# Retention's values of all four heads projected at once with the tokens on the partitions, heads of three tiles, and moved pieces, in a two-layer decoder trunk

## The reference

```python
h = rms_norm(x, g_mix[l])
z = h @ w_in[l]
qa, ka, va, ga, ub, vb, qc, kc, vc, gates = split_cols(z)
qa = rotary(qa.reshape(B, S, RET_HEADS, RET_DK), pos)
ka = rotary(ka.reshape(B, S, RET_HEADS, RET_DK), pos)
ya = retention(qa, ka, va.reshape(B, S, RET_HEADS, RET_DV))
ya = rms_normalize(ya) * ret_norm_g[l].reshape(RET_HEADS, RET_DV)
ya = silu(ga) * ya.reshape(B, S, RET_W)
...
x = x + merged @ w_o[l]
h = rms_norm(x, g_ffn[l])
gate, up = jnp.split(h @ w_gate_up[l], 2, axis=-1)
x = x + (silu(gate) * up) @ w_down[l]
```

## Time and profile before

| | us |
|---|---|
| median of 3 runs | 1914.49 (1914.34 to 1914.69) |
| the profiled execution's own time | 1913.97 |
| its span in the trace | 1912.2 |
| TensorE busy | 1896.2 (99%) |
| VectorE busy | 1246.9 (65%) |
| ScalarE busy | 843.6 (44%) |

### The profile page before, as it was taken

How to read it: one execution, slowest core, us unless ns; L and a number is a source line. 1 busy time by engine, 2 the same in 40 slices (tenths; PEclk the granted TensorE clock), 3 DMA queues, 4 the chain that set the end, 5 groups by cost and what they waited for, 6 DMA issues and landing times. The chain is left out here.

```text
span 1912.2 us, 26594 instructions
## 1 busy us (share of the span) xinstructions
PE 1896.2 (99%) x10632; PEld 1700.4 (89%) x10632; DVE 1246.9 (65%) x1625; ACT 843.6 (44%) x1186; POOL 97.2 (5%) x148
## 2 busy tenths in 40 slices
PE   8999999999999999999999999999999999999999
PEld 7888888888888899899888888888888888998998
DVE  7767767745656786377577677676365667863775
ACT  5544444424334455155345444345243444542554
POOL 0000001111111000000000000011111110000000
PEclk9999999999999999999999999999999999999999
DMA  5322347777777355366333222577777773553663
GB/s 202 91 75 73 85 130 185 191 203 217 211 199 212 100 168 177 100 187 198 123 100 94 67 78 81 148 197 190 208 205 199 201 205 100 180 160 107 203 209 123
DMA packets 85897, 295.68 MB, mean 155 GB/s; under 512 B 20368, under 2 KB 20624, under 8 KB 84624
## 3 DMA queue, kind: packets, MB, share of 16 engines
q1 hardware_dynamic: 73104, 218.49, 36.6%
q0 software_dynamic: 12672, 75.51, 17.5%
HBM read 291.79 MB, written 77.66 MB: 193 GB/s over the span
## 5 line engine op out<-in xcount | busy, mean ns | idle before, releaser
L1056 ACT ACTIVATE w_high<-raw 128x1024 fp32r<-128x1024 f32 x396 | 418.0, 1056 | 787.6 <-PE bank L846 663.5
L1262 DVE TENSOR_TENSOR w_low<-raw,w_high 128x1024 fp32r<-128x1024 f32 x396 | 482.8, 1222 | 148.7 <-ACT w_high L1056 142.8
L846 PE MATMUL bank<-h_high,w_high 128*128 128x512 f32 x1408 | 544.0, 386 | 9.0 <-DVE h_low L1267 8.3
L846 PE MATMUL bank<-h_low,w_high 128*128 128x512 f32 x1408 | 534.9, 380 | 0.0
L846 PE MATMUL bank<-h_high,w_low 128*128 128x512 f32 x1408 | 534.7, 380 | 0.0
L846 PEld LDWEIGHTS bank<-h_high,w_high 128*128 128x128 f32 x1408 | 267.0, 190 | 47.1 <-issue 8.2
L846 PEld LDWEIGHTS bank<-h_high,w_low 128*128 128x128 f32 x1408 | 266.8, 190 | 38.1
L846 PEld LDWEIGHTS bank<-h_low,w_high 128*128 128x128 f32 x1408 | 267.1, 190 | 36.4
L846 PE MATMUL bank<-in_high,w_high 128*128 128x512 f32 x672 | 255.0, 379 | 0.0
L846 PE MATMUL bank<-in_low,w_high 128*128 128x512 f32 x672 | 254.7, 379 | 0.0
L846 PE MATMUL bank<-in_high,w_low 128*128 128x512 f32 x672 | 254.7, 379 | 0.0
(11 more groups left out here) (163 smaller groups left out, 2345.5 us busy)
## 6 DMA issues: line engine op xcount, KB each, us to landing
raw<-weights SPq DMA_DIRECT2D x325, 512.0 KB, 4.1
weight_sums<-weights POOLq DMA_DIRECT2D x108, 512.0 KB, 6.3
raw<-weight_sums SPq DMA_DIRECT2D x72, 512.0 KB, 3.5
weight_sums<-weight_sums POOLq DMA_DIRECT2D x36, 512.0 KB, 4.0
turned<-rows SPq DMA_DIRECT2D x3, 768.0 KB, 7.6
xT<-x_t SPq DMA_DIRECT2D x8, 256.0 KB, 5.0
decay_sb<-decay SPq DMA_DIRECT2D x8, 256.0 KB, 4.8
out_t<-xT SPq DMA_DIRECT2D x8, 256.0 KB, 6.2
```

The lines of the kernel that those rows point to most:

```text
L846: return pe.matmul(o, w, m, start=start, stop=stop)
L1056: act.activation(w_high[:, PART_SLOT[s], :, :], raw[:, s % RAW_SLOTS, :, :], ACT.Copy).then_inc(part_high_w.sem, 1)
L1262: dve.tensor_tensor(w_low[:, PART_SLOT[s], :, :], raw[:, s % RAW_SLOTS, :, :], w_high[:, PART_SLOT[s], :, :], ALU.subtract).then_inc(part_ ...
```

## The change

The values of all four retention heads are four tiles (rv, 0) to (rv, 3) in a row ahead of the heads, projected like sv with the tokens on the partitions, into the banks 7, 6, 2 and the one of the tile before (`token_bank`), and copied out by ScalarE with the norm's factor per token. They live in places 10 and 11 of in_high and in_low. The heads are three tiles, rq, rk, rg, and their later steps come one tile earlier than before, counted from rq. The last dilated head's weighing, transposes and products lie beside the rv tiles and take the regular places. The decay has two buffers, the second in the place of a gate, and the loads for heads 0 and 1 are early. GpSimd starts at (rq, 0). The first loads on SP change places (third slab ahead of the identity), and the split of the third slab stands among the first squares. In the feed-forward, sums, high and low pieces stand in other places.

```diff
@@ tiles_of_layer
+    t += [("rv", j) for j in range(HEADS)]
     for h in range(HEADS):
-        t += [("rq", h), ("rk", h), ("rv", h), ("rg", h)]
+        t += [("rq", h), ("rk", h), ("rg", h)]
@@ schedule, heads
-        if h < HEADS - 1:
-            pre[t + 11] += [("weigh", h)]
-        if h < HEADS - 1:
-            pre[t + 12] += [("ptrans", h, 0), ("ptrans", h, 1)]
+        pre[t + 11] += [("weigh", h)]
+        pre[t + 12] += [("ptrans", h, 0), ("ptrans", h, 1)]
...
-        pre[t + 3] += [("vtrans", "rv", h)]
...
-        pre[t + 3] += [("rscore", h, m) for m in range(2)]
...
-        pre[t + 4] += [("rscore", h, m) for m in range(2, BLK)]
-        pre[t + 6] += [("rpv", h), ("ocopy", h), ("square", "r", h), ("split_sq", "r", h)]
-        pre[t + 7] += [("rowstat", "r", h), ("rowstd", "r", h)]
-        post[t + 7] += [("rowinv", "r", h)]
-        post[t + 8] += [("rowscale", "r", h), ("high", "yr", h), ("low", "yr", h)]
+        pre[t + 2] += [("rscore", h, m) for m in range(2)]
+        pre[t + 3] += [("rscore", h, m) for m in range(2, BLK)]
+        pre[t + 5] += [("rpv", h), ("ocopy", h), ("square", "r", h), ("split_sq", "r", h)]
+        pre[t + 6] += [("rowstat", "r", h), ("rowstd", "r", h)]
+        post[t + 6] += [("rowinv", "r", h)]
+        post[t + 7] += [("rowscale", "r", h), ("high", "yr", h), ("low", "yr", h)]
@@ schedule, feed-forward
-    post[AT["fgate", 0, 2]] += [("input_sum", "s1"), ("input_sum", "s2"), ("part_high", "s2")]
-    post[AT["fup", 0, 2]] += [("part_low", "s2"), ("part_high", "s1")]
-    post[AT["fgate", 0, 3]] += [("part_low", "s1"), ("input_sum", "s3"), ("part_high", "s3")]
+    post[AT["fgate", 0, 2]] += [("input_sum", "s1"), ("input_sum", "s2"), ("part_high", "s2"), ("part_high", "s1")]
+    post[AT["fup", 0, 2]] += [("part_low", "s2"), ("part_low", "s1"), ("input_sum", "s3")]
+    post[AT["fgate", 0, 3]] += [("part_high", "s3"), ("input_sum", "s4"), ("part_high", "s4"), ("part_low", "s3")]
...
-    post[AT["quick", PLAIN_PAIRS, A11B11]] += [("part_low", "s3"), ("input_sum", "s4"), ("part_high", "s4")]
-    post[AT["quick", PLAIN_PAIRS, S2T2]] += [("part_low", "s4"), ("part_high", "a22"), ("part_low", "a22")]
+    post[AT["quick", PLAIN_PAIRS, A11B11]] += [("part_high", "a22")]
+    post[AT["quick", PLAIN_PAIRS, S2T2]] += [("part_low", "s4")]
+    post[AT["quick", PLAIN_PAIRS, A12B21]] += [("part_low", "a22")]
@@ build
+        decays = [decay_sb[:, :], work[:, 18, :]]
...
+            return [stat_bank, out_bank, score_bank[0], bank_of(base, AT["rv", 0] - 1)]
@@ load_decay
-                if h > 0:
-
-                    sp.wait_ge(score_taken.sem, score_taken.at(base, "rscore", h - 1, BLK - 1))
-                sp.dma_start(decay_sb[:, :], decay[h]).then_inc(decay_loaded, 16)
+                if h > 1:
+                    sp.wait_ge(score_taken.sem, score_taken.at(base, "rscore", h - 2, BLK - 1))
+                sp.dma_start(decays[h % 2], decay[h]).then_inc(decay_loaded, 16)
@@ by_token
+                if role == "rv" and j == 0:
+                    pe.wait_ge(low_ready.sem, low_ready.at(base, "yc", HEADS - 2))
+                    pe.wait_ge(std_ready.sem, std_ready.at(base, "cq", HEADS - 1))
+                    pe.wait_ge(score_taken.sem, score_taken.at(base, "scores", HEADS - 1, 2))
...
+                        if role == "rv" and k == 0 and b == BLK - 1:
+                            wait_evacuated(pe, base, i - 1)
@@ rpv
-                        pe.wait_ge(v_stored.sem, v_stored.at(base, "rv", h))
+                        if h == 0:
+                            pe.wait_ge(values_ready.sem, values_ready.at(base, "rv", BLK - 1))
...
-                            last = matmul(out_bank[:, m * P:SEQ], ret_v[:, m, :], ret_s[:, RS_OFF[m]:RS_OFF[m] + SEQ - m * P],
+                            last = matmul(out_bank[:, m * P:SEQ], ret_v[m][:, h * P:(h + 1) * P], ret_s[:, RS_OFF[m]:RS_OFF[m] + SEQ - m * P],
@@ scalar, first squares (vector alike)
+                if n == 2:
+                    split(0, SPLIT_AHEAD)
```

More of the change, by code:

```diff
@@ L306, in schedule @@
             steps.append(("main", i, 0, len(BLOCKS[i])))
-        steps += splits + pre[i] + ([("evac", i)] if TILES[i][0] != "sv" else [("token_evac",)] if i == AT["sv", HEADS - 1] else [])
+        steps += splits + pre[i] + ([("evac", i)] if TILES[i][0] not in TOKEN_ROLES else
+                                [("token_evac", TILES[i][0])] if TILES[i][1] == HEADS - 1 else [])
         steps += later + post[i]
@@ L392, in build @@
         input_sum = over("input_sum", in_low_at + 4 * row_bytes, [P, 2, 4, 2 * P], F32)
+        ret_v_rows = [over("values_high", in_high_at + 10 * row_bytes, [P, 2, SEQ], F32),
+                      over("values_low", in_low_at + 10 * row_bytes, [P, 2, SEQ], F32)]
+        ret_v = [ret_v_rows[m // 2][:, m % 2, :] for m in range(BLK)]
         work_at = nc.sbuf_base
@@ L523, in build @@
         ret_copied = signal("ret_copied", keys("ocopy"))
-        values_ready = signal("spatial_values_ready", [(b,) for b in range(BLK)])
+        values_ready = signal("values_ready", [(role, b) for role in TOKEN_ROLES for b in range(BLK)])
         ln_var = signal("ln_var_ready", [()])
@@ L668, in build, with bank_number @@
         first_gate = gates[0]
+        def bank_number(base, i):
+            return (base // STRIDE * len(TILES) + i) % 2
         def bank_of(base, i):
@@ L702, in _ @@
             for layer in range(DEPTH):
-                pool.wait_ge(tile_stored.sem, tile_stored.at(layer * STRIDE, AT["rv", 0]))
+                pool.wait_ge(tile_stored.sem, tile_stored.at(layer * STRIDE, AT["rq", 0]))
                 for n, u in enumerate(QUICK_UNITS):
@@ L785, in read_pairs @@
                     pairs_swapped, 16)
-            decay_at = {behind(("k", 1, 0)): 0} | {load_behind("rscore", h - 1, BLK - 1): h
-                                                    for h in range(1, HEADS)}
+            decay_at = {behind(("k", h + 1, 0)): h for h in range(2)}
+            decay_at |= {load_behind("rscore", h - 2, BLK - 1): h for h in range(2, HEADS)}
             sp.dma_start(first_gain[:, :], gain_first).then_inc(first_gain_loaded, 16)
@@ L888, in main @@
             def main(base, i, first, end):
-                if TILES[i][0] == "sv":
+                if TILES[i][0] in TOKEN_ROLES:
                     by_token(base, i, TILES[i][1])
                     return
-                if i >= 2 * AHEAD_OF_NORM and first == 0:
+                if i == AT["rq", 0]:
+                    wait_evacuated(pe, base, AT["rv", 0] - 2)
+                elif i == AT["rk", 0]:
+                    pe.wait_ge(values_ready.sem, values_ready.at(base, "rv", BLK - 1))
+                elif i >= 2 * AHEAD_OF_NORM and first == 0:
                     wait_evacuated(pe, base, i - (4 if i < 3 * AHEAD_OF_NORM else
@@ L1080, in _ @@
                     if kind == "split_high":
-                        split(base, *key)
+                        if base > 0 or key[-1] != SPLIT_AHEAD:
+                            split(base, *key)
                     elif kind == "fill_ahead":
@@ L1133, in _ @@
                     elif kind == "token_evac":
-                        act.wait_ge(tile_done.sem, tile_done.at(base, AT["sv", HEADS - 1]))
+                        role, = key
+                        act.wait_ge(tile_done.sem, tile_done.at(base, AT[role, HEADS - 1]))
                         act.wait_ge(rstd_ready.sem, rstd_ready.at(base, "n", 0))
                         for b in range(BLK):
-                            act.activation(sg_v[:, b, :], token_bank[b][:, :], ACT.Gelu_apprx_tanh,
-                                           scale=rs[:, b:b + 1]).then_inc(values_ready.sem, 1)
+                            dst, func = (ret_v[b], ACT.Copy) if role == "rv" else (sg_v[:, b, :], ACT.Gelu_apprx_tanh)
+                            act.activation(dst, token_bank(base, role)[b][:, :], func, scale=rs[:, b:b + 1]).then_inc(
+                                values_ready.sem, 1)
                     elif kind == "square":
@@ L1277, in _ @@
                 sum_squares(dve, 0, 0, n)
+                if n == 1:
+                    split(0, SPLIT_AHEAD)
             for base in range(0, DEPTH * STRIDE, STRIDE):
@@ L1640, in _weights @@
                 src, col, row0 = w_down[layer], t[2] * P, t[1] * FF_BLOCKS[0] * P
-            elif t[0] == "sv":
+            elif t[0] in TOKEN_ROLES:
                 for s, place, i in blocks:
                     k, at = 2 * t[1] + i // 4, i % 4 * P
-                    values = w_in[layer][k * P:(k + 1) * P, of(("sv", 0)):of(("sv", 0)) + HEADS * P]
+                    values = w_in[layer][k * P:(k + 1) * P, of((t[0], 0)):of((t[0], 0)) + HEADS * P]
                     values = values.reshape(P, 2 * P, 2).transpose(0, 2, 1).reshape(P, HEADS * P)
```

37 lines of the change are left out of this document (17 added, 20 removed).

## The result

| us | before | after |
|---|---|---|
| median of 5 runs each | 1914.49 (1913.95 to 1914.77) | 1932.06 (1928.67 to 1934.24) |
| ratio | | 1.0090, 95% interval 1.0079 to 1.0101 |
| the profiled execution, its span | 1913.97, 1912.2 | 1928.67, 1926.9 |
| mean granted clock of each run | 1.000 (the profiled one) | 0.997, 0.995, 0.996, 0.996, 0.995 |

What follows compares the result with a forecast made beforehand. TensorE, busy 1896.2 of 1912.2 us, was taken as the bound. The terms -3.5 - 0.45 - 3.2 + 3.0 + 1.7 + 14.3 = +11.9 us on 1913.97 gave 1925.8, stated as 1926.0 us, range 1920.5 to 1932.

Steps and rivals of the forecast that it cites:

- the loop: Scores of one retention head to the next: VectorE's order makes TensorE idle 3.6 us before heads 2 and 3; +14.3 us.
- the rv tile: First rv tile: TensorE waits twice, for the scores' reader and the last v tile's evacuation; +3.0 us.
- the start: Program start: third slab's split moved ahead of six squares, costed at nothing; bounds 0 to 1 us.
- the first head: Scores wait for the late rotation of rk in the first head, 0.85 us a layer; +1.7 us.
- the pieces: Reordered pieces of the feed-forward input remove TensorE waits, 1.6 us a layer; -3.2 us.
- transposes and their wait: 32 value transposes dropped, -3.5 us, and the first one's wait behind the long weighing on VectorE, -0.45 us.
- Rival (b): Between heads, VectorE keeps up and rk is rotated by the end of rg's tile; 1910 us, chance 0.05.
- (c): Loop holds in part: heads 2 and 3 wait only 1.5 to 2 us; 1919 us, chance 0.08.
- The tail that I feared at the last fup tile: Feed-forward: late evacuation of the last fup tile makes the second product wait about 0.5 us.
- rival (a): Idle times ahead of heads 2 and 3 also throttle TensorE's clock; up to 12 us more, 1938, chance 0.12.

Runs made afterwards that it cites:

- kernel 1: Changed kernel plus 14 matmuls with overwritten results, filling TensorE's idle time before the rotated k of heads 2 and 3; 1924.63 us.
- kernel 7: Against kernel 6: norm factor multiplied into the rotation tables once a layer, rotation of rq and rk reads PSUM itself; 1905.99 us.
- kernel 4: The kernel before with the moved pieces of the feed-forward alone; 1911.68 us.
- kernel 3: Changed kernel with reciprocal, scaling and split of heads 0 and 1 behind the later head's rotations, and later waits in the first rv tile; 1913.01 us.
- kernel 6: Against kernel 3: low half of the last dilated head's product moved behind the first rotation of k; 1910.85 us.
- kernel 5: Against kernel 4: third slab loaded ahead of the identity and split ahead of six squares, on VectorE ahead of the first sum; 1910.51 us.
- kernel 8: Changed kernel with the reciprocal of heads 0 and 1 computed a second time into a free place; 1947.02 us.

## Why the prediction was right, and where it fell short

The sign and the mechanism held. The number, 1926.0, is 6.1 us below the median, which lies at the very edge of the range, 0.06 us past its upper end (1932.06 against 1932.0). The sum without the clock was nearly right (kernel 1, with the clock full, 1924.6), and a term that I had put down as a rival was missing from it. That the sum came so near is in part luck: the loop, the rv tile and the start came out 2.4 to 2.8 us below the forecast, the first head and the pieces 0.8 above. Step by step, for both layers:

| term | forecast | measured | by |
|---|---|---|---|
| transposes and their wait | -3.95 | -4.0 | kernel 7, its trace |
| pieces | -3.2 | -2.9 | kernel 4 |
| first rv tile | +3.0 | +2.2 to +2.6 | kernel 3 |
| first head | +1.7 | +2.2 | kernel 6 |
| loop, heads 2 and 3 | +14.3 | +13.5 | 4 x 3.37 |
| start | 0 (0 to 1) | -1.2, likely | kernel 5, whose start differs a little |
| clock | 0 | +7.4 | kernel 1 |

The measured column makes +17.2 to +17.6; the medians differ by 17.6.

**The loop.** TensorE's part of it came out as worked out: from the first score (310.63) to the small scores on VectorE (318.38) 7.75 us. VectorE's part took 15.76 us in place of 16.07, almost all of it in the stretch from the second evacuation to the low half of yr, 4.54 (326.79 to 331.33) in place of 4.91: read from the earlier trace rows that stretch held a wait of 0.96 us for ScalarE's high half, here 0.73, and a low half of 0.83 us, here 0.69. I had taken VectorE's starts in the old order as if nothing in them were waiting; one gap travelled with them. Rival (b), that VectorE keeps up, fell with the new waits and with kernel 8, where a microsecond more on VectorE was a microsecond more of waiting; (c) fell with the four stalls of 3.37 us, where it had 1.5 to 2.

**The pieces and the rv tile.** The tail that I feared at the last fup tile is there and of the size I gave it (idle 0.52 for 0.5). The first rv tile cost less mostly because the evacuation of the v tile took 1.34 us there and not 1.52.

**The start** was the one edit costed at nothing that wasn't nothing, by what the medians of kernels 4 and 5 suggest. The profiled run of before had the third slab's low half just in time, and so its trace showed no wait; one execution does not tell whether a margin is there or luck.

**The clock** is the step that failed. As rival (a) with a chance of 0.12 the clock was treated nearly as all or nothing, and as unlikely. It was neither: kernel 1 shows 7.4 us, more than half of rival (a)'s 12. "Nothing here tried it" was an argument for not knowing, and I read it as an argument against; with idle times four times the longest seen before, even odds on rival (a)'s 12 us and a forecast near 1932 would have been the honest sum. By the Trainium skill (TensorE: Matmul & The Clock Gate, HAM oscillation) a TensorE that waits is throttled again and pays on each return. Kernel 8 agrees, 6.4 us idle and a fall at each of four; the changed kernel only in part, with 3.21 us idle and a fall at two of four in its profile. In the six falls of the two profiles the clock fell 2.2 to 4.9 us into the idle time, so an idle time of 3.21 us can end before the fall comes. Why the moment varies is open: the four stalls have the same idle time, and what stands ahead of them is the same work. In how many stalls the other runs of the changed kernel lost the clock is open too, as only the mean clock of each is known.

## What to carry to other kernels

When the producer and its reader come closer by one tile, follow the loop through both engines, since shares of busy time (VectorE 78% here) don't show that the order puts a 3.4 us instruction ahead of the rotations of the next head, for which TensorE waits; then look for what can be ordered behind, which here was worth nearly all of the change's loss (16.8 of 17.6 us). Price every new idle time of TensorE as long as those seen here (3.2 us) with what the clock may take on top (1.5 to 3 us at each fall), and, where such a stall can't be removed, matmuls that fill it are worth having. Before taking a step that "just" fits from one profile as covered, look at how much margin it has.

## What was not expected of the hardware

- The same idle time of 3.21 us cost the clock in layer 1 (windows at 0.55 and 0.63) and not in layer 0 (1.00), in one execution; the five runs had mean clocks of 0.995 to 0.997. With 6.41 us it fell four times of four, and with waits of 1.4 us and less, in the other profiles, never. The falls came 2.2 to 4.9 us after TensorE's last work.
- How long TensorE still works at the lower level behind the idle time differs with the idle time the same: some 6.1 and 3.3 us in the changed kernel, 6.0, 3.4, 2.9 and 5.3 with the double reciprocal (twice what each window lost). A fall's price is so between 1.5 and 3 us.
- The clock column of the windows shows falls in the middle of the program (0.50), but not the slow start (1.00 for 8 matmuls at 0.43 us in the changed kernel, as in the earlier trace rows); there only the starts tell. The start's low stretch ended between 11.2 and 14.4 us in the ten profiled runs, by half of the difference an estimated 1.6 us at most from run to run.
